# Two chained transformer blocks on one core: modulation columns, attention-head work and a convolution placed elsewhere in the stream of weights

## The reference

```python
# first block, per layer
proj = modulate(rms_norm(x, w), sh1, sc1) @ w_in[l]
q, k, v, u_pool, ga, gp = split(proj)            # q, k normed per head, then rotated
merged = sigmoid(ga) * (attention(q, k, v) @ w_attn_o[l]) + sigmoid(gp) * pool
x = x + g1 * (merged @ w_out[l])
# second block, first layer: the same FFN weights on x and on the context
x   = norm(ALPHA * x   + 0.5 * gate * swiglu(modulate_2(x, ...)))
ctx = norm(ALPHA * ctx + 0.5 * gate * swiglu(modulate_2(ctx, ...)))
# second block, second layer
b_gate, c_gate, hv = split(h @ w_in, 3)
u = c_gate * hv
y = conv_w[0] * up[:, 0:n] + conv_w[1] * up[:, 1:n+1] + conv_w[2] * up[:, 2:n+2]
return (b_gate * y) @ w_out
```

## Time and profile before

| | |
|---|---|
| median of three runs | 3447.31 us (3447.08 to 3449.76) |
| the profiled execution, its own time | 3449.98 us |
| its span, granted TensorE clock | 3448.2 us, 0.996 of full speed |
| TensorE busy | 3381.9 us, 98% |
| VectorE busy | 2966.3 us, 86% |
| ScalarE busy | 2088.8 us, 61% |
| GpSimd busy | 210.4 us, 6% |
| bytes moved | 798.99 MB, 232 GB/s on the mean |

### The profile page before, as it was taken

One profiled execution on the slowest core, in us unless ns is written; L12 is line 12 of the kernel. 1 busy time (PEld: TensorE's weight loads), 2 busy tenths in 40 slices (PEclk: granted clock), 3 DMA queues, 4 the chain that ended last, 5 costly groups with the idle time before them and its releaser, 6 DMA issues.

```text
span 3448.2 us, 63008 instructions
## 1 busy us (share of the span) xinstructions
PE 3381.9 (98%) x21606; PEld 3029.3 (88%) x21606; DVE 2966.3 (86%) x6339; ACT 2088.8 (61%) x4400; POOL 210.4 (6%) x373
## 2 busy tenths in 40 slices
PE   9999999999999999999999999999999999999998
PEld 6989999988887988999998888998988788889887
DVE  7886989989988876989998988788888888888877
ACT  5554569965555564559985556544454755655555
POOL 0000111100000000111110000000001000000000
PEclk9999999999999999999999999999999999999999
DMA  8667666678886758776677777786766188687574
GB/s 320 206 229 233 226 217 195 192 256 294 282 288 207 250 172 265 226 228 195 192 233 264 269 266 236 241 272 227 252 226 230 47 275 271 226 266 226 178 238 152
DMA packets 250728, 798.99 MB, mean 232 GB/s; under 512 B 31472, under 2 KB 64240, under 8 KB 250368
## 3 DMA queue, kind: packets, MB, share of 16 engines
q1 hardware_dynamic: 230832, 738.82, 65.5%
q0 software_dynamic: 19664, 57.37, 4.9%
HBM read 759.87 MB, written 36.20 MB: 231 GB/s over the span
## 4 chain that ended last, share of the span: by engine, by line
PE 83%; DVE 11%; ACT 2%; DMA 2%; issue 2%; SPq 0%; DVEq 0%; ACTq 0%
PE bank L2752 12%; PE bank L2754 11%; PE bank L2753 11%; PE bank L2774 9%; PE bank L2867 8%; PE bank L2869 8%; PE bank L2868 8%; PE bank L2775 5%; DVE wl L1469 3%; PE bank L3160 2%; DMA raw<-stream 2%; PE bank L2777 1%; ACT wh L883 1%; DVE raw L1503 1%; PE bank L3143 1%
## 5 line engine op out<-in xcount | busy, mean ns | idle before, releaser
L883 ACT ACTIVATE wh<-raw 128x512 fp32r<-128x512 f32 x1916 | 1164.7, 629 | 803.9 <-PE bank L2869 347.6
L1469 DVE TENSOR_TENSOR wl<-raw,wh 128x512 fp32r<-128x512 f32 x1900 | 1257.5, 688 | 342.0 <-ACT wh L883 332.3
L2752 PE MATMUL bank<-XHL,wh 128*128 128x256 f32 x3104 | 888.7, 286 | 14.7 <-DVE wl L1469 10.1
L2754 PE MATMUL bank<-XHL,wl 128*128 128x256 f32 x3104 | 878.1, 283 | 0.0
L2753 PE MATMUL bank<-XHL,wh 128*128 128x256 f32 x3104 | 877.7, 283 | 0.0
L2752 PEld LDWEIGHTS bank<-XHL,wh 128*128 128x128 f32 x3104 | 593.0, 191 | 29.7 <-DVE wl L1469 12.2
L2753 PEld LDWEIGHTS bank<-XHL,wh 128*128 128x128 f32 x3104 | 593.6, 191 | 0.8
L2754 PEld LDWEIGHTS bank<-XHL,wl 128*128 128x128 f32 x3104 | 593.5, 191 | 0.0
L2867 PE MATMUL bank<-wh,AH 128*128 128x512 f32 x1464 | 574.6, 392 | 3.7 <-DVE wl L1469 0.9
L2868 PE MATMUL bank<-wl,AH 128*128 128x512 f32 x1464 | 570.5, 390 | 0.0
L2869 PE MATMUL bank<-wh,AL 128*128 128x512 f32 x1464 | 570.2, 389 | 0.0
(11 more groups left out here) (345 smaller groups left out, 4845.5 us busy)
## 6 DMA issues: line engine op xcount, KB each, us to landing
raw<-stream SPq DMA_DIRECT2D x1316, 512.0 KB, 4.5
side<-h_spill SPq DMA_DIRECT2D x256, 128.0 KB, 4.7
h_spill<-side POOLq DMA_DIRECT2D x252, 128.0 KB, 3.7
arena<-stream SPq DMA_DIRECT2D x24, 512.0 KB, 15.1
arena<-norm_rows POOLq DMA_DIRECT2D x40, 128.0 KB, 4.7
arena<-rpb POOLq DMA_DIRECT2D x16, 256.0 KB, 5.7
arena<-gate_spill POOLq DMA_DIRECT2D x10, 256.0 KB, 5.1
X<-x_t SPq DMA_DIRECT2D x2, 512.0 KB, 5.2
```

Of the source, the lines that this page charges most:

```text
L883: act.activation(wh[:, n % 4, :], raw[:, q % 4, HALF * half:HALF * (half + 1)], ACT.Copy).then_inc(hi_ready, 1)
L1469: tt_op(wl[:, n % 4, :], raw[:, q % 4, HALF * half:HALF * (half + 1)], wh[:, n % 4, :].bitcast(F32), SUB).then_inc(lo_ready, 1)
L2752: pe.matmul(out, wh[:, n % 4, a:b], moving_h, start=start, stop=False, skip_group_check=check)
L2754: return pe.matmul(out, wl[:, n % 4, a:b], moving_h, start=False, stop=stop, skip_group_check=check)
```

## The change

**The table of columns.** Each column still gets folded once, elsewhere. In the first layer, the five columns behind attention heads are gone; `w_in.0` has nine columns instead of six (three of the new ones behind units 22 to 27), and `w_out.0` has one behind each of its eight units instead of behind six. In `w_in.1` the eleven columns leave the key rows (units 10 and 11) for later units. In `ffn.0.0` there are 16 wide columns instead of 14, at pairs 1, 3, 4, 6 and 8 in place of 2, 3 and 4; in `ffn.0.0.x` the pairs 0 and 2 have none behind their row unit, and the second column of a pair stands at pairs 8, 9, 10, 14 and 20 instead of 1, 2, 3, 4 and 7. Three of its columns are wide now, before five. In `conv_in` the six columns stand three units apart, before two.

**Context pass.** The hooks of `ffn.0.0.x` on VectorE and ScalarE move a pair later, but for TensorE's sum of squares; the mean over rows now stands behind the row unit of pair 1. The masks of the attention bias (L2421 now) go to pairs 3, 5, 6 and 15 to 19, before 13 to 20.

**Casts first.** In `w_in` ScalarE now casts the next unit before it does head work (argument `beside`); layer 1 casts unit 9 after two squares instead of after four, and VectorE makes the low half of unit 10 between the two sums of squares.

**Convolution.** Units of `conv_in` come as triples (`c_gate`, `hv`, `b_gate` of one group), so one group is convolved per three units. The next operand goes into its own pair `conv_pair` while `conv_in` still runs, the buffer is cleared only at its edges, the gate row is ordered in two halves, the base steps go one pair per triple, and the four filler matmuls are gone.

```diff
-            put("w_in.1", (8, 10, 11, 12, 14, 16, 18, 20, 23, 25, 30), name, columns[5:16])
+            put("w_in.1", (8, 12, 14, 16, 18, 20, 22, 24, 26, 27, 30), name, columns[5:16])
...
-            put("w_out.0", range(1, 7), name, columns[18:24])
+            put("w_out.0", range(KT), name, columns[16:24])
...
-            if (name, k) == ("attn_o.0", 0):
-                order += [("fold1.0", FIRST_FOLDS + 11 + n) for n in range(len(HEAD_FOLDS))]
...
+CONV_ORDER = [KT * part + k for k in range(KT) for part in (1, 2, 0)]
...
             def step(k, i, per):
                 hi(st, k + 1, i, per)
+                if beside is not None:
+                    beside()
                 take(k, i, per)
...
             group_done(st, ROW_UNITS - 1)
+            product(st, to_arena(PROJ), 12, 13, beside=keys_and_values)
+            product(st, to_arena(PROJ), 13, 14, beside=last_queries_and_key_roots)
+            product(st, to_arena(PROJ), 14, 15, beside=lambda: normed_heads(1, range(4, 8)))
+            product(st, to_arena(PROJ), 15, 16, beside=normed_keys)
...
-        hooks = {-1: lambda: copy_sum(stages["ffn.0.0"]), 0: lambda: sum_rows(ctx_tiles, 1), 1: lambda: centre(ctx_tiles),
-                 3: lambda: sum_squares(2), 6: context_inverse, 7: lambda: context_normed(0), 8: lambda: context_normed(1)}
+        hooks = {-1: lambda: copy_sum(stages["ffn.0.0"]), 1: lambda: sum_rows(ctx_tiles, 1), 2: lambda: centre(ctx_tiles),
+                 4: lambda: sum_squares(2), 7: context_inverse, 8: lambda: context_normed(0), 9: lambda: context_normed(1)}
...
+        for edge in (0, T + 1):
+            step(dve.memset(cu[:, :, edge:edge + 1], 0.0))
+        for unit in range(4, 3 * KT):
+            product(st, None, unit - 1, unit)
+            k, part = divmod(unit - 4, 3)
+            if part == 0:
+                if k:
+                    rest((k - 1,), modul, pair=conv_pair)
                 convolve(k)
+            if part == 2 and k < 4:
+                base_steps(k)
...
         pe.wait_ge(group_free, 2 + stages["conv_in"].g + 2)
-        keep_busy(4, banks[0])
-        projection_rows(stages["conv_o"], 0, KT)
+        projection_rows(stages["conv_o"], 0, KT, conv_pair)
```

More of the change, by code:

```diff
@@ L119, in folds_after @@
     put("expert_v.1", FOLDED_BESIDE_VALUES[1], "fold2", two[EARLY_COLUMNS:21])
-    put("ffn.0.0", rows_of((2, 3, 4) + tuple(range(10, 21))), "fold2", two[21:35])
-    put("ffn.0.0.x", rows_of(range(21)), "fold2", two[35:40] + two[48:64])
-    put("ffn.0.0.x", [3 + 3 * j for j in (1, 2, 3, 4, 7)], "fold2", two[64:69])
+    put("ffn.0.0", rows_of((1, 3, 4, 6, 8) + tuple(range(10, 21))), "fold2", two[21:37])
+    put("ffn.0.0.x", rows_of((3, 5, 6)), "fold2", two[37:40])
+    put("ffn.0.0.x", rows_of((1, 4) + tuple(range(7, 21))), "fold2", two[48:64])
+    put("ffn.0.0.x", [3 + 3 * j for j in (8, 9, 10, 14, 20)], "fold2", two[64:69])
     put("kv_ctx", (5, 6, 8, 10), "fold2", two[69:73])
@@ L126, in folds_after @@
     put("ffn.1.0", rows_of(range(21)), "fold2", two[109:130])
-    put("conv_in", range(5, 17, 2), "fold2", two[130:136])
+    put("conv_in", range(5, 21, 3), "fold2", two[130:136])
     put("ffn.1.1", rows_of(range(8)), "fold2", two[136:144])
@@ L419, in build @@
     PR2, PT2 = 10240, 12288
[L420 removed]
+    CONV, CU, CT, CONV_OPERAND = 16384, 2048, 4352, 22528
     GATE_ROW, GATE_SPREAD = 0, 1024
@@ L896, in group_done, with product @@
             act.wait_ge(halves_free, SLOTS + 2 * (st.s + k + 1) + 2 * per * i)
-        def product(st, evacuate=None, a=0, b=None, then=None, opened=False, both=False):
+        def product(st, evacuate=None, a=0, b=None, then=None, opened=False, both=False, beside=None):
             b = st.units if b is None else b
@@ L1434, in _ @@
         boundary(2)
-        st = stages["conv_o"]
-        product(stages["conv_in"], to_arena(CONV), 0, 20, opened=True)
-        order_gate(3)
-        product(stages["conv_in"], to_arena(CONV), 20, 24, then=st)
-        operand((0, 1), modul)
-        for k in range(2, KT):
-            product(st, None, k - 2, k - 1)
-            operand((k,), modul)
-        product(st, None, KT - 2, KT, then=stages["ffn.1.1"], both=True)
+        st, co, keep = stages["conv_in"], stages["conv_o"], to_arena(CONV)
+        product(st, keep, 0, 5, opened=True)
+        for k in range(KT - 2):
+            product(st, keep, 3 * k + 5, 3 * k + 6, beside=lambda: operand((k,), modul, pair=conv_pair))
+            if k in (3, 4):
+                product(st, keep, 3 * k + 6, 3 * k + 7, beside=lambda: order_half_gate(3, k - 3))
+            else:
+                product(st, keep, 3 * k + 6, 3 * k + 7)
+            product(st, keep, 3 * k + 7, 3 * k + 8)
+        operand((KT - 2,), modul, pair=conv_pair)
+        product(st, keep, 23, 24, then=co)
+        product(co, None, 0, 2)
+        operand((KT - 1,), modul, pair=conv_pair)
+        product(co, None, 2, KT, then=stages["ffn.1.1"], both=True)
         boundary(3)
@@ L2662, in _, with projected @@
         boundary(stages["ffn.1.0"], 2, stages["conv_in"])
[L2664 removed]
+        st, co = stages["conv_in"], stages["conv_o"]
         cu, conv = tiles(CU, KT, T + 2), tiles(CT, KT)
[L2666 to L2679 removed]
+        def projected(k, part):
+            return A(CONV + (3 * k + part) * T, T)
         def convolve(k):
[L2682 to L2683 removed]
+            dve.wait_ge(group_free, 2 + st.g + 3 * k + 3)
+            step(tt_op(cu[:, k, 1:1 + T], projected(k, 0), projected(k, 1), MUL))
             settle()
```

129 lines of the change are left out of this document (56 added, 73 removed).

## The result

Measured: 3428.8 us median (3426.43 to 3430.4, five runs) against 3447.08 for the kernel before on the same chip (3445.12 to 3449.76, five runs). The ratio is 0.9948, with a 95% interval of 0.9936 to 0.9959: 18.3 us less, half a percent, with the interval clear of 1; 18.9 less was forecast for an execution like the profiled one. The profiled execution took 3429.86 us (span 3428.1), 20.1 less than the profiled one of before.

The account below looks back on a forecast made before the run. TensorE, busy 98% of the span, bounds the kernel, so time comes only from its waits, mostly for VectorE's low halves. Seven terms sum to -18.9 us: 3431.1 against the profiled execution, 3428.4 against the median; range 3421 to 3439.

Parts of the forecast that it names:

- the two slow stretches (2.95): Context pass: clock 0.50 for 3.4 us behind each of two gaps, 2.95 us lost for both.
- w_in.0: Two of four waits go as casts precede ScalarE's head work: -1.4 us, ends 0 and -2.4; three added columns covered.
- heads: Head stage of layer 0 loses its five columns and matches layer 1's 18.90 us: -2.3, ends -1.9 to -2.4.
- w_out.0: Eight columns: about 0.5 lost behind unit 0, 0.9 for two more columns' loads; +1.4 us, from 0.3 to 3.
- my ring formula: w_out.0: landing time 6.52 plus 1.9 of work, halved, 4.2 us per unit over 2.88; only last units feel it.
- w_in.1: Casts between squares and columns off the key rows take all waits but one: -3.9 us, ends -2.5 and -4.3.
- ffn.0.0: Wait of 1.3 at pair 2 goes, new ones of 0.8 and 1.6 at pairs 6 and 8: +1.2, ends -1.3 and +3.
- ffn.0.0.x: Context pass, the largest term: waits and slow clock go, about 2 us left: -8, ends -6 and -9.5.
- the 9.9 us to win: Context pass: four waits, 7.0 us with 0.16 each, and 2.95 for the slow clock.
- Convolution: Idle time, fillers and six waits, 6 us, nearly all go: -5.9, ends -4 and -6.5.
- Half given back: Rival: moved columns meet other VectorE steps, ten waits come back, 8.6 us, so 3437; 3434 to 3440 had chance 0.19.
- The ring: Rival: loads landing in 7.49 us at 24 places with a column per unit; 24 us slower, 3471; chance 0.03.

Follow-up runs that it names:

- after_again: The changed kernel once more, unedited, on the same chip as the two mended ones; 3429.31 us, 0.9950 of before.
- run both: Changed kernel with w_out.0 back to six columns, w_in.0 eleven, and the ffn.0.0 columns of pairs 6 and 8 placed elsewhere; 3426.97 us, 0.9942 of before.
- moved_again: As the run both, with the narrow column of pair 7 of the context pass moved to pair 2; 3426.58 us, 0.9943 of before.
- x_columns_old: Changed kernel with the columns of ffn.0.0 and ffn.0.0.x where they were before, hooks still a pair later; 3428.8 us.

## Why the prediction was right, point by point

**What bounds the kernel.** Right: VectorE's work is the same, and the time followed TensorE's waits. Of the 20.1 us between the two spans 11.8 are idle time of TensorE; 8.3 are busy time, the two slow stretches (2.95), the fillers (about 1) and what each wait adds to the matmul behind it.

**w_in.0, heads.** Right, with their mechanism: the waits of 0.87 and 0.57 went and came back with the casts alone; the comparison of layer 0 with layer 1 gave the heads to 0.05 us.

**w_out.0.** Right in sign and in cause (the loads); +1.4 was forecast, +1.1 measured over all traces. How it is made up was wrong: the 0.5 for the column behind unit 0 didn't come, no wait stands there in the profiled trace. And my ring formula, which has only the last units feel a late load, was too simple. The profiled trace has 1.12 us idle in the middle of the stage and 0.60 at its end, after_again 0.48 and 0.16, with the same instructions.

**w_in.1.** -4.5 in the two profiled traces, just beyond the lower end -4.3, and -3.9 over all traces, the forecast. The wait of 1.82 us for the late load, which I had counted whole, was 0.69 and 0.51 in the two other traces that have it, so the term was worked out from an execution in which it was long. The mechanism is shown, but for the share of the late load (see the experiment).

**ffn.0.0.** The two new waits came out within 0.1 us. The sum is 0.4 lower in the two profiled traces since a wait at pair 13 for a load (0.7 in the trace of before) is absent in the one after. That isn't the change's doing: the three other traces with the columns of before don't have it either, and over all traces the stage is 1.6 longer, 0.4 more than forecast.

**ffn.0.0.x.** -8.3 for -8. Of the 9.9 us to win I left 2 over; 1.4 are left (0.51, 0.50 and one more of 0.4), which makes 8.5. The 0.2 between is open. The runs with fillers show that of the 9.9 the clock alone is worth 2.3, not 2.95: the rest of it can be won only together with the wait behind it.

**Convolution.** -6.6 for -5.9 (end -6.5) in the two profiled traces, -5.9 over all. The wait of 1.6 us (1.43 idle) for a load beside the gate's broadcast, of which I kept some, went altogether; but it was 0.34 idle in the two other traces that have it, so 1.1 of it was chance.

**The rivals.** Half given back: it happened in places (ffn.0.0, w_out.0), up to 3.9 us in all, and these were in the forecast. The ring: loads of 6.65 us did occur in w_out.0, but the stage costs about 1.1 us more and not the 14 of this rival; the ring starts full and is refilled in the next stage. The run both shows the same mechanism deciding a place (1.9 us), so it was a rival with real force and a price put some ten times too high.

**How much of the match is luck.** In the two profiled traces the seven stages give -21.5, and 1.4 came back in stretches that the change doesn't touch, 1.0 of it at the start (see the last section). Over all traces they give -19.4, each within 0.5 us of its term, so the terms didn't meet the total by cancelling large errors. That the medians came within 0.6 us of the forecast is luck: five executions of one kernel lie up to 4.6 us apart.

## What to carry to other kernels

Where one engine is full on the mean and another waits for it, look for what stands behind one and the same unit: two steps that each fit cost little apart and more than their sum together, since the wait grows to gaps like those behind which TensorE's clock fell here. Compare stages over several traces: one trace of before had two waits for loads that were 1.1 to 1.3 us longer than in the others. Compare a stage with the same stage in another layer before reckoning. Before a transfer is moved to where an engine is idle, look at the ring too: idle time that waits for a load is no room.

## What the runs showed of the hardware

The same gap doesn't always lower the clock. Near 2660 us (2672 in the kernel before) each of fourteen profiled executions of these kernels has an idle gap of 1.84 us at the same instruction. Behind it the granted clock was 0.50 in seven and 1.00 in the other seven. TensorE and the window right behind, first the changed kernel, then the run both:

```profile
2659.49 0.70 PE L3268 MATMUL bank<-arena 64*128 64x256 f32 x2 [1.84 <-ACT arena L1418]
```

```profile
2661.00:2664.40 3.40, 3.40 (x20) 2.67 (x20) 3.33 (x10) 3.02 (x8) 0.00 (x0) 0.50 0.00 0
```

```profile
2659.80:2663.20 3.40, 3.36 (x34) 2.40 (x32) 3.33 (x10) 3.03 (x9) 0.00 (x0) 1.00 0.00 0
```

No wait stands right behind this gap to hide the loss, so here is what a slow stretch costs. The 68 matmuls about the gap take 9.53 to 9.54 us in the seven executions without one, 11.00 to 11.14 in six with one of 3.41 us, and 12.39 in moved_again, where it is 6.83 long: about 1.5 us for each 3.41. A window within the last:

```profile
2655.40:2662.20 6.80, 6.80 (x34) 4.95 (x35) 4.99 (x14) 5.27 (x14) 0.00 (x0) 0.50 0.00 0
```

Gaps of 1.97, 2.10, 2.15 and 2.41 us in the context pass each had a half clock behind them, four of four; waits of 1.0 to 1.7 idle there had none, nor had the 1.82 in w_in.1 of the kernel before. The first 48 us of the program, with waits of up to 4.3 us, take 45.1 to 47.5 us from the first matmul in the eleven executions of the changed kernel and its variants. The three longest (47.1 to 47.5) had 6.8 us at 0.50 in them; the two with none took 45.1 and 46.1.

The stretch between the context pass and the convolution, which no edit here touches, takes 600.0 to 605.1 us, 1.5 or 3 of it by this clock. These two stretches vary by 2.4 and 5.1 us, where the five runs of the changed kernel span 4.0 (3426.43 to 3430.4), and are the main reason why the single time of x_columns_old showed nothing where its trace shows two changes of -1.7 and +6.1.
